# A two-layer diffusion trunk on one core: the order of the first loads in the value phase, and the output product of the chunked scan

## The reference, cut to what matters

```python
u = u_tab[it]
v = v_tab[it]
act = jax.nn.gelu(jnp.einsum("tkd,td->tk", u, xt), approximate=False)
return jnp.einsum("tk,tkd->td", gt * act, v)
```

```python
xdt = x * dt[..., None]
cb = jnp.einsum("bclgn,bcsgn->bgcls", Cc, Bc)
m = cb[:, :, None] * jnp.exp(segsum(dA))
y_diag = jnp.einsum("bgrcls,bcsgrp->bclgrp", m, xdt)
```

## Time and profile before

| | us |
|---|---|
| median of three runs | 4649.47 (4649.28 to 4654.41) |
| the profiled execution | 4651.51 |
| its span, first to last instruction | 4649.9 |
| TensorE busy in the span | 4162.9 (90%) |
| VectorE busy | 3280.0 (71%) |
| ScalarE busy | 1596.4 (34%) |
| POOL busy | 1927.7 (41%) |

### The profile page before, as it was taken

The page is one execution under the profiler, slowest core; times in us unless marked ns, Lnnn a source line. Parts: engine busy times, 40 slices in busy tenths (PEclk is TensorE's granted clock), DMA queues, the critical chain, the costliest instruction groups (busy, mean ns, idle before and its releaser), DMA issues. The chain is left out here.

```text
span 4649.9 us, 60093 instructions
## 1 busy us (share of the span) xinstructions
PE 4162.9 (90%) x21972; PEld 3757.0 (81%) x21972; DVE 3280.0 (71%) x5896; ACT 1596.4 (34%) x2831; POOL 1927.7 (41%) x1108
## 2 busy tenths in 40 slices
PE   6979999899969999969899798799999996999997
PEld 6868888899958888847677678688888996888886
DVE  3869788798858778836656642227887995778776
ACT  2121333377723223222222222213335774223222
POOL 1213466665435445401121232136666553445452
PEclk8989999999989999989999899899999998999998
DMA  5535465699899999800101021125568998999994
GB/s 192 192 140 198 153 218 201 230 382 365 334 334 351 349 361 360 320 19 36 43 25 45 32 73 50 66 87 185 202 213 308 366 367 305 358 354 354 353 360 160
DMA packets 402216, 1051.17 MB, mean 226 GB/s; under 512 B 23440, under 2 KB 203920, under 8 KB 396816
## 3 DMA queue, kind: packets, MB, share of 16 engines
q1 hardware_dynamic: 290064, 642.62, 38.4%
q0 software_dynamic: 112000, 406.90, 24.1%
HBM read 921.36 MB, written 127.40 MB: 226 GB/s over the span
## 5 line engine op out<-in xcount | busy, mean ns | idle before, releaser
L418 PE MATMUL ov_p<-acts_p,wide_v_p 128*128 128x448 f32 x6144 | 1280.3, 370 | 126.9 <-DVE acts_p L1394 126.9
L418 PEld LDWEIGHTS ov_p<-acts_p,wide_v_p 128*128 128x128 f32 x6144 | 1166.8, 190 | 240.0 <-issue 83.4
L418 PE MATMUL he_p<-h_p,wide_early_p 128*128 128x448 f32 x3456 | 720.8, 370 | 52.2 <-POOL wide_early_p L862 50.1
L418 PEld LDWEIGHTS he_p<-h_p,wide_early_p 128*128 128x128 f32 x3456 | 658.7, 192 | 108.9 <-issue 53.4
L418 PE MATMUL hl_p<-h_p,wide_late_p 128*128 128x448 f32 x2688 | 577.9, 371 | 15.5 <-DVE wide_late_p L1242 15.5
L418 PEld LDWEIGHTS hl_p<-h_p,wide_late_p 128*128 128x128 f32 x2688 | 501.1, 190 | 53.6 <-issue 15.9
L862 POOL TENSOR_TENSOR wide_early_p<-ring,wide_early_p 128x1024 fp32r<-128x1024 f32 x144 | 374.4, 2601 | 319.8 <-ACT wide_early_p L924 319.5
L1365 ACT ACTIVATE acts_p<-hidden_in_p 128x448 fp32r<-128x448 f32 x256 | 148.0, 578 | 848.5 <-DVE hidden_in_p L1390 848.1
L1390 DVE TENSOR_TENSOR hidden_in_p<-hidden_in_p,gbuf_p 128x448 f32<-128x448 f32 x256 | 158.0, 617 | 302.9 <-DMA hidden_in_p<-hidden 302.9
L1112 DVE SCALAR_TENSOR_TENSOR acc_p<-rows_v_p,weight_p,acc_p 128x1024 f32<-128x1024 f32 x286 | 365.6, 1278 | 6.7
L1094 POOL DMA_INDIRECT rows_v_p<-in_v,ids_p x160 | 237.7, 1485 | 253.8 <-DVE acc_p L1112 203.8
(11 more groups left out here) (297 smaller groups left out, 6618.9 us busy)
## 6 DMA issues: line engine op xcount, KB each, us to landing
ring<-in_stream SPq DMA_DIRECT2D x162, 2048.0 KB, 11.0
gates<-staged_p SPq DMA_DIRECT2D x28, 2048.0 KB, 8.2
gbuf_p<-gates SPq DMA_DIRECT2D x64, 896.0 KB, 16.9
hidden_in_p<-hidden SPq DMA_DIRECT2D x64, 896.0 KB, 18.8
hidden<-gelu_early_p SPq DMA_DIRECT2D x144, 224.0 KB
hidden<-gelu_late_p SPq DMA_DIRECT2D x112, 224.0 KB, 4.7
ada_ineven_in<-in_ada_rows SPq DMA_DIRECT2D x16, 1024.0 KB, 5.0
ada_inq<-in_ada_rows SPq DMA_DIRECT2D x16, 1024.0 KB, 5.0
```

The source lines that it names most:

```text
L418: last = nc.tensor.matmul(out, lhsT=w, rhs=rhs[:, c, part, cols_], start=start and n == 0, stop=stop and n == 2)
```

## The change

In the value phase SP issues factors 0 first; the reload of xT goes behind the factors of group 9. POOL waits for factors 0 before its first gather.

In the scan `dt` moves from x to the score matrix: ScalarE scales the backward-masked matrix by each head's backward `dt` (four copies, `backward`), VectorE adds the forward-masked one times the forward `dt` (four instructions), and one product with E gives `mix`, so that one output product per head, with x itself, does for both directions. `xdt` and its memset go. Two semaphores are new: ScalarE waits for the masks (`masked`), VectorE for ScalarE (`back`). Block 3 of the next group moves from tile 1 to tile 3 on TensorE, and its copy on ScalarE behind the last exponent.

```diff
--- before.py
+++ after.py
@@ -1308,17 +1308,19 @@
                             sp.dma_start(hidden[:, j, :, :], hidden_dram[at_:at_ + GROUP].rearrange("b p t -> p b t"))\
                               .then_inc(factors_in[j], 16)
 
-                        sp.dma_start(xT[:, :, :], x_park).then_inc(x_back, 16)
                         load_factors(0)
                         for g in range(N // GROUP):
                             if g + 1 < N // GROUP:
                                 load_factors(g + 1)
+                            if g == 8:
+                                sp.dma_start(xT[:, :, :], x_park).then_inc(x_back, 16)
                             if first + SLOTS + g * GROUP < N_BLOCKS:
                                 sp.wait_ge(blocks_used, first + (g + 1) * GROUP)
                                 load_half(sp, g % 2, first + SLOTS + g * GROUP)
 
                     @block.gpsimd
                     def _(pool):
+                        pool.wait_ge(factors_in[0], 32)
                         for k in range(len(rows_in.jobs)):
                             rows_in.fetch(pool, units, k, jobs_done)
 
@@ -1557,13 +1559,13 @@
                 xch = sb("xch", [P, 2, TOK], into=ph)
                 bc = sb("bc", [P, 2, 2, TOK], into=ph)
                 tokm = sb("tokm", [P, TILES, 3 * P], into=ph)
-                xdt = sb("xdt", [P, 2, 2, GW + YN - HEADDIM], into=ph)
                 xw = sb("xw", [P, 4, GW], into=ph)
                 xD = sb("xD", [P, GW], into=ph)
                 spans = sb("spans", [P, 2, HPG, P], into=ph)
                 E = sb("E", [P, HPG, P], into=ph)
                 CBm = sb("CBm", [P, 2, P], into=ph)
-                mix = sb("mix", [P, 2, 2, HPG, P], into=ph)
+                CBdt = sb("CBdt", [P, HPG, P], into=ph)
+                mix = sb("mix", [P, 2, HPG, P], into=ph)
                 off = sb("off", [P, 2, GW], into=ph)
                 SF = sb("SF", [P, SAMPLE_TILES, GW], into=ph)
                 SB = sb("SB", [P, SAMPLE_TILES, GW], into=ph)
@@ -1580,7 +1582,7 @@
                 S = {n: sem("scan_" + n) for n in (
                     "init_in", "proj", "copied", "conved", "silued", "turned", "turned_out", "weighted", "spanned",
                     "seg", "exped", "cb", "cb_used", "mixed", "y", "y_used", "off", "st", "st_used", "states",
-                    "final", "final_out", "last_free", "dma_turns")}
+                    "final", "final_out", "last_free", "dma_turns", "masked", "back")}
 
                 def groups(eng, body):
 
@@ -1695,7 +1697,7 @@
                             for t in range(TILES):
                                 if t + 1 < TILES:
                                     cb_and_seg(n, j, t + 1)
-                                if t == 1:
+                                if t == 3:
                                     next_block(3)
                                 tok = slice(t * P, (t + 1) * P)
                                 pe.wait_ge(S["y_used"], n(TILES, t + 1))
@@ -1707,9 +1709,8 @@
                                 for h in range(HPG):
 
                                     out = p_y[:, h * HEADDIM:h * HEADDIM + YN]
-                                    for d in range(2):
-                                        last = mm(out, lhsT=mix[:, t % 2, d, h, :], rhs=xdt[:, t % 2, d, h * HEADDIM:h * HEADDIM + YN],
-                                                  start=d == 0, stop=d == 1)
+                                    last = mm(out, lhsT=mix[:, t % 2, h, :], rhs=tokm[:, t, h * HEADDIM:h * HEADDIM + YN],
+                                              start=True, stop=True)
                                 last.then_inc(S["y"], 1)
 
                         for b in range(4):
@@ -1761,7 +1762,15 @@
                                 next_copy(b)
                                 next_silu(b)
 
+                            def backward(t):
+                                act.wait_ge(S["masked"], n(TILES, t + 1))
+                                for h in range(HPG):
+                                    last = a(CBdt[:, h, :], CBm[:, 1, :], ACT.Copy,
+                                             scale=dt[:, t, bass.ds(n(HPG, HEADS + h), 1)])
+                                last.then_inc(S["back"], 1)
+
                             def exp(t):
+                                backward(t)
                                 act.wait_ge(S["seg"], n(TILES, t + 2))
                                 act.wait_ge(S["mixed"], n(TILES, t + 1))
                                 a(E[:, :, :].rearrange("p h l -> p (h l)"), p_seg[:, :], ACT.Exp).then_inc(S["exped"], 1)
@@ -1771,9 +1780,9 @@
                             exp(1)
                             next_silu(2)
                             exp(2)
-                            next_copy(3)
                             exp(3)
                             exp(4)
+                            next_copy(3)
 
                         for b in range(4):
                             copy_block(lambda per, k: k, b, 0)
@@ -1787,7 +1796,6 @@
                         D = dve_steps
                         heads = lambda ap: ap.rearrange("p (h q) -> p h q", h=HPG)
                         D.did(v.memset(upad[:, :, :], 0.0))
-                        D.did(v.memset(xdt[:, :, :, :], 0.0))
                         D.settle(dve)
 
                         for name, k in (("conved", 2), ("st_used", 4), ("cb_used", 1), ("mixed", 1), ("y_used", 1)):
@@ -1854,20 +1862,21 @@
                             def weights(t):
 
 
-                                for d in range(2):
-                                    D.did(v.tensor_tensor(heads(xdt[:, t % 2, d, 0:GW]), heads(tokm[:, t, 0:GW]),
-                                                          hd(dt, t, d * HEADS), ALU.mult))
                                 dve.wait_ge(S["cb"], n(TILES, t + 1))
                                 dve.wait_ge(S["mixed"], n(TILES, t + 1))
                                 D.did(v.tensor_tensor(CBm[:, 0, :], p_cb[:, 0:P], masks[:, LE, :], ALU.mult))
                                 D.did(v.tensor_tensor(CBm[:, 1, :], p_cb[:, 0:P], masks[:, GE, :], ALU.mult))
                                 D.settle(dve)
                                 dve.sem_inc(S["cb_used"], 1)
+                                dve.sem_inc(S["masked"], 1)
+                                dt_of = lambda d, h: dt[:, t, bass.ds(n(HPG, d * HEADS + h), 1)]
+                                dve.wait_ge(S["back"], n(TILES, t + 1))
+                                for h in range(HPG):
+                                    D.did(v.scalar_tensor_tensor(CBdt[:, h, :], in0=CBm[:, 0, :], scalar=dt_of(0, h),
+                                                                 in1=CBdt[:, h, :], op0=ALU.mult, op1=ALU.add))
+                                D.settle(dve)
                                 dve.wait_ge(S["exped"], n(TILES, t + 2))
-                                for d in range(2):
-                                    last = v.tensor_tensor(mix[:, t % 2, d, :, :], E[:, :, :], bcast(CBm[:, d, :], 1, HPG),
-                                                           ALU.mult)
-                                last.then_inc(S["mixed"], 1)
+                                v.tensor_tensor(mix[:, t % 2, :, :], E[:, :, :], CBdt[:, :, :], ALU.mult).then_inc(S["mixed"], 1)
 
                             weights(0)
                             for t in range(TILES):
@@ -1893,7 +1902,7 @@
                                 v.tensor_tensor(y_out_t, p_y[:, 0:GW], xD[:, :], ALU.add).then_inc(S["y_used"], 1)
 
                         CONV = 4 * 3
-                        GROUP = 6 * 2 + 2 + TILES * 5 + SAMPLE_TILES * 4
+                        GROUP = 6 * 2 + 2 + TILES * (3 + HPG) + SAMPLE_TILES * 4
                         for b in range(3):
                             conv_block(lambda per, k: k, b, 0)
                         with D.loop(dve, GROUPS_ // 2 - 1, 2 * (GROUP + CONV)) as r:
```

## The result

The changed kernel takes 4666.48 us (median of seven runs, 4661.24 to 4674.47) against 4649.47: ratio 1.0037, 95% interval 1.0027 to 1.0046. That is 17 us **slower**, past the 0.2%, where 4647.8 and no change were forecast; the time lies inside the range. The profiled execution took 4669.73 us (span 4668.2, granted clock 0.94).

What follows compares the result with a forecast made beforehand. Value phase paced by DMA bytes; in the scan TensorE mostly busy, waiting for VectorE's outputs in the tail. 4651.5 - 18.5 + 16.8 = 4649.8, or 4647.8 us against the runs' median; range 4620 to 4676.

Steps and rivals of the forecast that it cites:

- Value phase, 18.5: Value phase, both layers: idle DMA time gets filled, 7.7 + 1.7 + 7.4 + 1.7 = 18.5 us less.
- the term of 1.7 us a layer for xT's return: Value phase: xT's reload lands in a small DMA gap (share 0.71), adding 1.7 us to each layer's gain.
- Scan, 16.8: Scan: each of seven groups with the moved block takes 2.4 us longer, 16.8 us more in all.
- Output 0 ends 0.7 us earlier: Scan group: mixture ends at 2282.2, convolution and output 0 follow unchanged, so output 0 ends at 2288.2 instead of 2288.87.
- TensorE waits about 4 us at tile 1: Scan, tile 1: with the block gone, TensorE, through with tile 0 by 2284.31, waits about 4 us until 2288.2.
- The sum ended at the group's first transposition: Scan: one group's path was summed to the next group's start, 2313.8 instead of 2311.35, 2.4 us later.
- The eighth group zero: Scan, last group, without such a block: longer tile chain against a shorter last product, taken as zero.
- the four signs of being wrong: Wrong if: group's period falls; tile-1 wait under 2 us; tiles 1-2 clock 0.50; value phase keeps over 12 us/layer.
- Clock: Scan: low clock from tile 1's wait to the block costs 3.3 us a group, 4671 us; chance 0.20.
- The scan breaks even: Scan: unstretched VectorE and full clock through the group's end leave 0.1 us a group, 4632 us; chance 0.20.
- The head start holds: Value phase: head start kept but for xT's own time, 32 us in place of 18.5, 4634 us; chance 0.10.
- Order without effect: Value phase: same bytes due, the idle stretch only moves, 0 in place of 18.5, 4666 us; chance 0.05.

Runs made afterwards that it cites:

- e2: The kernel before with the change's scan edits alone, value phase as before: 4681.14 us, ratio 1.0073.
- e1: The kernel before with the change's value-phase edits alone, scan as before: 4634.10 us, ratio 0.9974.
- e4: The kernel before with the last projection block at tile 3 and its copy behind the last exponent, two products per head kept: 4675.31 us.
- e7: The changed kernel with 16 products nobody reads (32 records, 8.78 us) in TensorE's wait at tile 1: 4668.55 us.
- e15: The changed kernel with block 3 at tile 1, masks and dt joined before the scores exist, one VectorE product replacing two masked matrices: 4621.60 us.
- e13: The changed kernel with 5 products nobody reads in TensorE's wait before a group's last output products: 4660.94 us.

## Why the prediction was wrong

The forecast was a difference of two terms, -18.5 and +16.8. Both had the right sign, and the mechanism of the second was the one that came: TensorE idle at tile 1, and the block without cover at tile 3. Its size was about half of what came, 31.8 us by e2's time and 38.4 in the trace.

**Value phase, 18.5.** In the changed kernel's trace it is 12.3, by e1's time 15.2. The idle DMA time is filled as forecast: the share that was 0.23 and 0.18 is 1.04 and 1.03. What failed is the term of 1.7 us a layer for xT's return: VectorE waits 11.0 us for the eleventh factors there, 7.8 at the same place before, so the return cost 3.2 us and filled no gap. The third factors came 12.1 us earlier (8 to 15 expected); the first gating at 9.3 us, not 20. POOL's wait was given a part in the gain that it does not have beside xT's move.

**Scan, 16.8.** In the group that the prediction followed, from the end of ScalarE's block copy to the next group's first transposition, it was 2311.35 - 2278.57 = 32.78 us and is 2314.02 - 2277.10 = 36.92: 4.1 more, where 2.4 was forecast (3.5 as the mean of the groups). Step by step:
- *Output 0 ends 0.7 us earlier*: **this step failed first**. 2288.87 - 2278.57 = 10.30 us became 2288.35 - 2277.10 = 11.25, 0.95 later. Costing tile 1's fused products at a mix of stretched and unstretched, I put the end of the mixture 3.6 us after the copy (2282.2 - 2278.57); it came after 4.8, since they took 2.51 us, past even my upper end of 1.74. The convolution and output behind it, which I took as unchanged, need 6.44 us instead of 5.95. These 1.65 us are the way from 2.4 to 4.1.
- *TensorE waits about 4 us at tile 1*: 5.79, nearly all by the same miss.
- *Tile 1 7.2 us*: 2295.52 - 2288.35 = 7.17. *To the block 4.5*: 2299.97 - 2295.52 = 4.45. *Block 8.78*: 8.78. *Tail 5.1*: 2314.02 - 2308.75 = 5.27. These held, and so did ScalarE's copies at 1.28 (1.22 to 1.56).
- **The sum ended at the group's first transposition**, and this failed with more weight. What follows was taken as unchanged and costs 1.6 us a group: 1.1 by the clock, as half of the time at 0.50 (4.9 against 2.7 us), and 0.5 before the first state product.
- *The eighth group zero*: from its second score product to its last output 34.63 against 31.94 us, 2.7 more: without a block the longer tile chain is not hidden by anything.

As means of the groups: (3.5 + 1.6) x 7 + 2.7 = 38.4, the measured difference of the scans. Of the 21.6 us that the sum lacks, the tiles are (3.5 - 2.4) x 7 = 7.7, the next group's start 11.2 and the eighth group 2.7. A part of the 11.2 belongs to this pair of traces: the time at 0.50 is 2.5 to 4.1 us a group in the four traces with the scan of before, 4.5 to 4.9 in the four with the whole block at tile 3 and no filler in the tail (changed, e2, e4, e7).

**The signs and the rivals.** Three of the four signs of being wrong did not show, and the fourth only in part: the clock was 0.50 behind the wait in tile 1, but 1.00 in tile 2. *Clock* was right that a low clock costs, with the size (3.3 us a group) too large, and in the wrong place: behind the wait half clock costs nothing (e7), at the next group's start about 1 us. The Trainium skill, "TensorE: Matmul & The Clock Gate", Why this matters for your kernels, asks for no idle gaps between bursts of products; the rows agree that the clock falls behind them (0.50), and show that the price depends on whether TensorE is dense where it falls. *The scan breaks even* took the block at tile 3 as a gain for the clock in the tail: it was up there, and down afterwards. *The head start holds* fell, 12 of 22 us were left by the third factors. *Order without effect* fell by e1; that its 4666 us is the time measured is chance. The single chances as listed add up to 0.36 for the same time and 0.28 for slower, not 0.35 and 0.29.

What stays open: why xT and the gathers together delay the factors by 22 us, when each alone costs 6 and 2 us, and why VectorE's loop turns later when the block is at tile 3. Neither was tried.

## What to carry to other kernels

Before moving a long piece of work, ask what it covers where it stands: here a block beside another engine's longest stretch was free (2 of its 8.78 us showed in the kernel before), and the test is to put a useless one there (e7). Follow a moved piece into the next iteration, since the low-clock stretch moved with the waits. Work that depends on masks and scales alone can be joined before the scores exist (e15), and here that gave 17 us, about as much as the whole value-phase half.

## What was not expected of the hardware

GpSimd's span products stretch VectorE's fused products of 128x128 from 347 to 1124 ns; with GpSimd doing no arithmetic the longest is 354. A low-clock stretch of 3.4 to 17.1 us comes around the start of each group (the second to the seventh) in every trace but e13's, where two groups have none. Between the first state product and the score product of tile 0 it cost exactly half of its length (20.72 to 20.78 us plus that half, in 108 groups of 18 traces); behind the wait at tile 1 it cost nothing. The factors' loading time behind one or two other streams is far from additive (9.3, 11.3, 15.3 and 31.5 us).
